# Split weights side by side in one buffer per slot, at two starting bytes for 512-wide and 256-wide products, and another order of work in the third feed-forward panel

## What is computed

```python
def swiglu(h, w_gate, w_up, w_down):
    return (jax.nn.silu(h @ w_gate) * (h @ w_up)) @ w_down
...
    x = x + nsa_pool_mixer(rmsnorm(x, mix_norm[0]), ...)       # layer 1: projections, attention, output projection
    x = x + swiglu(rmsnorm(x, ffn_norm[0]), ...)               # hidden width 2816
    x = x + conformer_conv(rmsnorm(x, mix_norm[1]), ...)       # layer 2: two projections around a convolution
    x = x + swiglu(rmsnorm(x, ffn_norm[1]), ...)
    h = rmsnorm(x, final_norm)                                 # then the second block, layer 3
    h = h + concatenate([gated_linear_attention, short_conv]) @ w_out
    h = h + (silu(a) * bb) @ w_down                            # third feed-forward
    h = h + sigmoid(rmsnorm(h, ln3_g) @ w_ple_gate) * (p @ w_ple_proj)
    return _rmsnorm(h, lnf_g)
```

## Time and profile before

| | us |
|---|---|
| median of three runs | 1771.36 |
| the profiled execution's own time | 1770.64 |
| its span | 1768.9 |
| PE busy in the span | 1713.2 (97%) |
| DVE busy | 1260.3 (71%) |
| ACT busy | 863.4 (49%) |
| POOL busy | 517.6 (29%) |

### The profile page before, as it was taken

One profiled execution on the slowest core, in us unless ns is written; L12 is line 12 of the kernel. 1 busy time (PEld: TensorE's weight loads), 2 busy tenths in 40 slices (PEclk: granted clock), 3 DMA queues, 4 the chain that ended last, 5 costly groups with the idle time before them and its releaser, 6 DMA issues.

```text
span 1768.9 us, 27531 instructions
## 1 busy us (share of the span) xinstructions
PE 1713.2 (97%) x10662; PEld 1480.4 (84%) x10662; DVE 1260.3 (71%) x1756; ACT 863.4 (49%) x1310; POOL 517.6 (29%) x356
## 2 busy tenths in 40 slices
PE   8999999999999999999999999999999999999997
PEld 6767789988998865789988998788778898899876
DVE  8667687854875798788845776588757875487565
ACT  5338557733763312547723764433335673277342
POOL 1342124602540246225503540023301560254000
PEclk9899999999999999999999999999999999999998
DMA  6210223333332565223433332322212333333332
GB/s 215 85 48 1 73 72 96 99 105 107 96 113 82 130 155 145 73 72 96 114 107 90 107 106 77 124 72 72 73 63 79 94 98 107 107 96 100 104 97 70
DMA packets 284698, 168.99 MB, mean 96 GB/s; under 512 B 8288, under 2 KB 278528, under 8 KB 284576
## 3 DMA queue, kind: packets, MB, share of 16 engines
q1 hardware_dynamic: 283664, 165.10, 33.2%
q0 software_dynamic: 624, 1.67, 0.3%
q10 hardware_dynamic: 288, 0.54, 0.1%
HBM read 156.59 MB, written 2.10 MB: 90 GB/s over the span
## 4 chain that ended last, share of the span: by engine, by line
PE 82%; DVE 11%; ACT 3%; issue 2%; POOL 1%; DMA 0%; DVEq 0%; SPq 0%; ACTq 0%; POOLq 0%
PE ps L1342 32%; PE ps L1027 14%; PE ps L1028 14%; PE ps L1029 14%; DVE wlo L1646 2%; PE ps L1423 1%; ACT whi L602 1%; PE ps L1268 1%; PE ps L1225 1%; DVE ps L2179 1%; DVE rstd L1688 1%; PE ps L1250 1%; DVE act_lo L1678 1%; DVE wlo L1959 1%; DVE tt L1975 1%
## 5 line engine op out<-in xcount | busy, mean ns | idle before, releaser
L1027 PE MATMUL ps<-act_hi,whi 128*128 128x512 f32 x796 | 320.7, 403 | 17.7 <-DVE act_lo L1678 8.6
L1029 PE MATMUL ps<-act_hi,wlo 128*128 128x512 f32 x796 | 315.1, 396 | 0.0
L1028 PE MATMUL ps<-act_lo,whi 128*128 128x512 f32 x796 | 314.1, 395 | 0.0
L602 ACT ACTIVATE whi<-raw 128x2048 fp32r<-128x2048 f32 (+3 forms) x104 | 166.9, 1605 | 233.6 <-PE ps L1029 219.5
L1646 DVE TENSOR_TENSOR wlo<-raw,whi 128x2048 fp32r<-128x2048 f32 (+3 forms) x96 | 191.1, 1990 | 42.4 <-ACT whi L602 42.0
L1342 PE MATMUL ps<-act_hi,whi 128*128 128x256 f32 x720 | 200.7, 279 | 10.9 <-ACT ps L773 6.8
L444 POOL TENSOR_TENSOR raw<-raw 128x512 f32<-128x512 f32 x60 | 82.0, 1367 | 433.1 <-DVE sqacc L1666 177.8
L1028 PE MATMUL ps<-hid_lo,whi 128*128 128x512 f32 x528 | 207.7, 393 | 0.0
L1027 PE MATMUL ps<-hid_hi,whi 128*128 128x512 f32 x528 | 206.3, 391 | 0.0
L1029 PE MATMUL ps<-hid_hi,wlo 128*128 128x512 f32 x528 | 205.9, 390 | 0.0
L1027 PEld LDWEIGHTS ps<-act_hi,whi 128*128 128x128 f32 x796 | 151.4, 190 | 62.4 <-issue 21.6
(11 more groups left out here) (402 smaller groups left out, 3919.7 us busy)
## 6 DMA issues: line engine op xcount, KB each, us to landing
raw<-in_ffn_w_gate_dram SPq DMA_DIRECT2D x44, 512.0 KB, 4.0
raw<-in_ffn_w_up_dram SPq DMA_DIRECT2D x44, 512.0 KB, 5.3
raw<-in_w_gate_upffn_dram SPq DMA_DIRECT2D x44, 512.0 KB, 4.6
raw<-in_ffn_w_down_dram SPq DMA_DIRECT2D x32, 384.0 KB, 4.2
raw<-in_conv_w_pw_dram SPq DMA_DIRECT2D x24, 512.0 KB, 5.7
raw<-in_w_in_dram SPq DMA_DIRECT2D x24, 512.0 KB, 4.5
raw<-in_ffn_w_down_dram SPq DMA_DIRECT2D x32, 320.0 KB, 3.6
z<-z SPq DMA_DIRECT2D x28, 262.0 KB, 5.0
```

Source lines behind the costliest of these rows:

```text
L602: act.activation(whi[:, n % 2, 0:cols], raw[:, n % 2, 0:cols], ACT.Copy).then_inc(hi_done, 1)
L1027: pe.matmul(out, lhs[0], rhs[0], start=start, stop=False)
L1028: pe.matmul(out, lhs[0], rhs[1], start=False, stop=False)
L1029: return pe.matmul(out, lhs[1], rhs[0], start=False, stop=stop)
```

## The change

It does four things. It replaces `whi` and `wlo` by one buffer per slot, `w0` and `w1`, which holds the high part and, 8192 bytes on, the low part. It starts them 48 elements (192 bytes) into the buffer for products by `mm3` and at its beginning for products of the seven-product scheme. It moves other buffers so that the starts come out at chosen bytes: `ones` is one column (a broadcast makes the rest), `eps6`, `eps5` and `wtap` come later, 96 bytes stand unused ahead of `w0`, `ssum` goes ahead of `sw_hi`, and 320 bytes ahead of that. And it orders the third panel otherwise. By the same rule of sizes `w0` then starts at byte 72448, `w1` at 89344, `act_hi` at 105920 as before, `sw_hi` at 216832 and `sw_lo` at 222976; `act_*`, `hid_*` and `bt_*` keep their bytes.

```diff
+SKEW = 48
-        whi = sb("whi", [P, 2, SLOT], F32R)
-        wlo = sb("wlo", [P, 2, SLOT], F32R)
-        ones = sb("ones", [P, P])
+        ones = sb("ones", [P, 1])
-        eps6 = sb("eps6", [P, 1])
-        eps5 = sb("eps5", [P, 1])
         t3 = sb("t3", [P, 2, S])
+        sb("pad_w", [P, 24])
+        w0 = sb("w0", [P, SKEW + 2 * SLOT], F32R)
+        eps6 = sb("eps6", [P, 1])
+        eps5 = sb("eps5", [P, 1])
         wtap = sb("wtap", [P, 2, CONV])
+        w1 = sb("w1", [P, SKEW + 2 * SLOT], F32R)
+        def w_of(n, skew=SKEW):
+            w = (w0, w1)[n % 2]
+            return w[:, skew:skew + SLOT], w[:, skew + SLOT:skew + 2 * SLOT]
...
-            ("bt_lo", [P, 3, Q4, HALF], F32R), ("sw_hi", [P, 3, Q4 * P], F32R), ("sw_lo", [P, 3, Q4 * P], F32R),
-            ("ssum", [P, 2, Q4 * P], F32),
+            ("bt_lo", [P, 3, Q4, HALF], F32R), ("ssum", [P, 2, Q4 * P], F32), ("pad_sw", [P, 80], F32),
+            ("sw_hi", [P, 3, Q4 * P], F32R), ("sw_lo", [P, 3, Q4 * P], F32R),
...
-                act.activation(whi[:, n % 2], raw[:, n % 2], ACT.Copy).then_inc(hi_done, 1)
+                act.activation(w_of(n, 0)[0], raw[:, n % 2], ACT.Copy).then_inc(hi_done, 1)
...
                             cast_hidden(u - 1)
                             hi_sum(u + 1, n + 1, dn, 0)
+                            hi_sum(u + 1, n + 1, dn, 1)
+                            continue
+                        if k == 2:
+                            take(u, dn, 0)
+                            hi_sum(u, n, dn, 2)
+                            silu(u - 1)
+                            take(u, dn, 1)
+                            hi_panel(u + 1, n + 1)
+                            take(u, dn, 2)
+                            act.wait_ge(panel_done, n)
+                            cast(combo("T4")[0], tt4[:, :, :], "bt_hi")
+                            cast_hidden(u - 1)
+                            hi_sum(u + 1, n + 1, dn, 0)
                             continue
...
-            def slot(n, k, width=256, c0=0):
+            def slot(n, k, width=256, c0=0, skew=SKEW):
                 a = slice(k * width + c0, k * width + c0 + P)
-                return whi[:, n % 2, a], wlo[:, n % 2, a]
+                return tuple(w[:, a] for w in w_of(n, skew))
...
-                pe.matmul(ps[4][:, :], ones[:, :], sqacc[:, :], start=True, stop=True).then_inc(sem("sumsq"), 1)
+                pe.matmul(ps[4][:, :], ones[:, :].broadcast_to([P, P]), sqacc[:, :], start=True, stop=True).then_inc(sem("sumsq"), 1)
...
-                return lambda k: slot(n, c * Q4 + k, P)
+                return lambda k: slot(n, c * Q4 + k, P, skew=0)
...
                         if k == 2:
+                            lo_sum(u, dn, 1)
                             whole_gate(u - 1, n - 1)
-                            lo_sum(u, dn, 1)
                             lo_sum(u, dn, 2)
+                            whole_hidden(u - 1)
+                            gate_first(u)
+                            lo_panel(u + 1, n + 1)
                             low(combo("T4")[1], tt4[:, :, :], combo("T4")[0], "bt_hi", 4 * f + 4, "bt_lo")
-                            whole_hidden(u - 1)
-                            lo_panel(u + 1, n + 1)
-                            low_hidden(u - 1)
-                            gate_first(u)
-                            gate_second(u)
                             continue
                         if k > ks[0]:
                             up_second(u - 1)
+                            if k == 3:
+                                gate_second(u - 1)
+                                low_hidden(u - 2)
...
-            ve.tensor_scalar(minus[:, :], ones[:, :], -1.0 / P, None, ALU.mult)
+            ve.memset(minus[:, :].bitcast(F32), -1.0 / P)
```

More of the change, by code:

```diff
@@ L217, in program @@
         kvc = pc_t = pt[:, 0:2 * S].rearrange("p (j t) -> p j t", j=2)
-        hid_hi, hid_lo, bt_hi, bt_lo, sw_hi, sw_lo, ssum = region([
+        hid_hi, hid_lo, bt_hi, bt_lo, ssum, _, sw_hi, sw_lo = region([
             ("hid_hi", [P, 12, S], F32R), ("hid_lo", [P, 12, S], F32R), ("bt_hi", [P, 3, Q4, HALF], F32R),
-            ("bt_lo", [P, 3, Q4, HALF], F32R), ("sw_hi", [P, 3, Q4 * P], F32R), ("sw_lo", [P, 3, Q4 * P], F32R),
-            ("ssum", [P, 2, Q4 * P], F32),
+            ("bt_lo", [P, 3, Q4, HALF], F32R), ("ssum", [P, 2, Q4 * P], F32), ("pad_sw", [P, 80], F32),
+            ("sw_hi", [P, 3, Q4 * P], F32R), ("sw_lo", [P, 3, Q4 * P], F32R),
         ])
@@ L516, in diagonals @@
                 pool.wait_ge(split_done, n)
-                pool.tensor_tensor(wlo[:, n % 2], raw[:, n % 2], whi[:, n % 2].bitcast(F32), ALU.subtract)\
+                w_hi, w_lo = w_of(n)
+                pool.tensor_tensor(w_lo, raw[:, n % 2], w_hi.bitcast(F32), ALU.subtract)\
                     .then_inc(split_done, 1)
@@ L601, in hi @@
                     act.wait_ge(panel_done, 2 * i + (n - 1))
-                act.activation(whi[:, n % 2, 0:cols], raw[:, n % 2, 0:cols], ACT.Copy).then_inc(hi_done, 1)
+                act.activation(w_of(n)[0][:, 0:cols], raw[:, n % 2, 0:cols], ACT.Copy).then_inc(hi_done, 1)
             def square(q, k, src, kk=None):
@@ L633, in _ @@
                 a = slice(half * SLOT // 2, (half + 1) * SLOT // 2)
-                act.activation(whi[:, 0, a], raw[:, 0, a], ACT.Copy).then_inc(hi_done if half else sem("w0_hi"), 1)
+                act.activation(w_of(0)[0][:, a], raw[:, 0, a], ACT.Copy).then_inc(hi_done if half else sem("w0_hi"), 1)
                 for k in range(4 * half, 4 * half + 4):
@@ L829, in ffn @@
                         take(u, dn, 0)
-                        if k == 2:
-                            act.wait_ge(panel_done, n)
-                            cast(combo("T4")[0], tt4[:, :, :], "bt_hi")
                         if not first:
@@ L1645, in lo @@
                 a = slice(0, cols)
-                ve.tensor_tensor(wlo[:, n % 2, a], raw[:, n % 2, a], whi[:, n % 2, a].bitcast(F32), ALU.subtract)\
+                w_hi, w_lo = w_of(n)
+                ve.tensor_tensor(w_lo[:, a], raw[:, n % 2, a], w_hi[:, a].bitcast(F32), ALU.subtract)\
                     .then_inc(split_done, 1)
@@ L1709, in _ @@
             ve.wait_ge(sem("gains_in"), 16)
+            w_hi, w_lo = w_of(0)
             for half in range(2):
@@ L1712, in _ @@
                 ve.wait_ge(hi_done if half else sem("w0_hi"), 1)
-                ve.tensor_tensor(wlo[:, 0, a], raw[:, 0, a], whi[:, 0, a].bitcast(F32), ALU.subtract)\
+                ve.tensor_tensor(w_lo[:, a], raw[:, 0, a], w_hi[:, a].bitcast(F32), ALU.subtract)\
                     .then_inc(split_done if half else sem("w0_lo"), 1)
@@ L1958, in lo_panel @@
                 ve.wait_ge(hi_done, n + 1)
-                ve.tensor_tensor(wlo[:, n % 2], raw[:, n % 2], whi[:, n % 2].bitcast(F32), ALU.subtract)\
+                w_hi, w_lo = w_of(n, 0)
+                ve.tensor_tensor(w_lo, raw[:, n % 2], w_hi.bitcast(F32), ALU.subtract)\
                     .then_inc(sem("up_split"), 1)
```

## The result

The changed kernel took 1754.35 us (median of four, 1753.50 to 1754.95) beside 1772.31 us of the kernel before (1770.56 to 1774.29): ratio 0.9898, 95% interval 0.9886 to 0.9909. It is faster by 18 us where 38 were forecast, inside the range and on the right side. On a second chip the same kernel took 1763.11 us against 1772.96 (ratio 0.9942, 0.9925 to 0.9959), and the difference between the two chips turns out to belong to the explanation.

What follows compares the result with a forecast made beforehand. PE was taken as the bound, busy 1713.2 of 1768.9 us. Gains of 9.9 + 14.4 + 0 + 13.5 = 37.8 us took the profiled 1770.6 to 1732.8, median 1733.5, rounded 1733; range 1702 to 1762.

Steps and rivals of the forecast that it cites:

- Part 1: Third up panel of each feed-forward: the new ACT and DVE order removes most lost time, 3.3 us each, 9.9 in all.
- Part 2: 256-wide matmuls on the sums' weights (`sw_*`): distance 0 to 320 shortens the step from 120.0 to 113.3 ns, 14.4 us.
- Part 3: The panels' own 256-wide matmuls: moving from distance 192 to 320 leaves the step at 113.3 ns, no change in time.
- Part 4: 512-wide matmuls: moving from distance 192 to 0 shortens the mean step from 229.0 to 225.5 ns, 13.5 us gained.
- (a): 512-wide step falls to 220 ns, gaining 35.7 us, with 256-wide ones at 111.8 ns: 1704 us; chance 22%.
- (b): 512-wide matmuls cost the same at distance 0 as at 192, so no gain there: 1747 us; chance 20%.
- (c): Buffer place does nothing and `sw_*` is slow for another reason; only the third panel's order gains: 1761.5 us; chance 7%.
- (d): 256-wide matmuls: distance 320 is as bad as 0, own ones lose 19.3 us, 1780.8 us, deciding from 116.7 ns; chance 6%.
- (e): Third panel's new order stalls elsewhere, `lo_panel` above all, and gives 2 us or less, the rest holding: 1741 us; chance 4%.
- The rule of two ports: PE reads moving operand and weights through independent ports and never waits; by it Parts 2 to 4 are worth nothing.

## Why the prediction came out half right

- **Part 1, 9.9 us: right.** The order alone gave 9.2 us in the traces (7 to 8 by the times). The wait for `take` 1 is gone, the clock dip with it, and the third panel came out at 9.03 us where about 9.3 was forecast.
- **Part 2, 14.4 us: right by itself, wrong in this change.** "I take 113.3, the step that the other nonzero distance has" holds for distance 320 with the own matmuls at 192 (14 us measured). In the change the mean was 116.5: 2160 x 3.5 = 7.6 us.
- **Part 3, nothing: this is the step that failed.** "I take no change" cost 2880 x 2.6 = 7.5 us in the trace of the result and 2880 x 3.7 = 10.7 on the second chip. What part 2 gave, part 3 took. The working took a step to be a property of a distance. The runs show two steps, 113.3 and 117.8, at the very same distance, and what decides is what came before: the last wait or delay, or the last change of distance. With every product at 320 there is none of the latter left. The row that could have told was in the trace: the kernel before has 31 groups at 117.8 at distance 192. That every panel of before brought its own matmuls back to 113.3 behind a stretch at 120 was read as waste alone.
- **Part 4, 13.5 us: mechanism right, size off.** A step of 225.5 was taken; it is 227.0, and 3972 x 1.96 = 7.8 us. The 226.6 named in the text, "the same excess here", was the better choice: the uniform step in the steady state is 226.7. Of the three differing steps of a product, the shortest was taken, and equal ones came, near their mean less 2. Two sums of this part are also off: 229.0 less 225.5 is 3.5 and not 3.4 ns, and no excess at all would be 3972 x 15.7 = 62 us and not 58.
- **Sum:** 9.2 + 7.6 - 7.5 + 7.8 = 17.1 us. The medians differ by 18.0, the profiled spans by 16.0, so the terms account for the change to about 1 us. Beside the forecast, 7.5 us are missing by part 3, 6.8 by part 2, 5.7 by part 4 and 0.7 by part 1. That the sum came out at half of the forecast and not lower is in part luck: on the second chip the same kernel gave 9.9.
- **Rivals.** (a) is out at every distance tried. (b) and (c) are out, 512 columns gained and the place counts. (d) is half true: the own matmuls lost, up to 117.6 on the second chip, beyond its deciding 116.7, but the sums and the 512-wide gained with it. (e) did not occur.
- **The rule of two ports.** The Trainium skill (SBUF — State Buffer, "Who interferes with whom") has PE wait on nobody. The runs disagree by up to 6.7 ns a matmul, with nothing altered but start bytes: 120.0 at distance 0 and 113.3 at 192 in one panel, and 1754 or 1763 us (by the chip) becomes 1746 on a third chip by 128 bytes. Whether the two reads of SBUF meet or something behind them does is not shown by any run here.

## What to carry to other kernels

Where PE is the bound and every matmul has fresh weights, measure the step from start to start in each stretch, by the start bytes of both operands modulo 512, and look for stretches of one form with two steps. Place the weights so that neighbouring products differ in distance in a way that leads to the short step (here 192 and 320 in turn). One distance throughout was not enough where it was tried, at 320; 192 throughout is untried. Compare variants by traces and on more than one chip, since the steps that waits and delays leave behind made some 6 of the 12 us between two profiled executions of one kernel.

## What the runs showed of the hardware

- At 256 columns: 120.0 ns at distance 0 and, once settled, at 256; 118.1 in the mean at 128 and 384 for the sums' weights, from 112 to 124 singly; 117.8 nearly always at 64; 113.3 or 117.8 at 192, 320 and 448. At 512 columns: 226.7 at 0 and 256, 229 at 192 and 448, 232 to 234 at 64, 128, 320 and 384. The order of good and bad turns round with the width. In every 256-wide case the moving operand stood at remainder 448, so there no run tells the distance from the weights' own remainder.
- 113.3 and 117.8 are each held over hundreds of matmuls. A wait, a single step lengthened by 15 to 50 ns, or a change of distance can move PE from one to the other, though not each time; between these one change was seen in some 17,700 matmuls. Why there are two is open.
